# Residual product as four 64x64 blocks, a twentieth home for weight pieces, and three key tiles ahead of the transposes

## The chip, the cores and the metric

One core of a Trainium2 chip runs the whole kernel in one launch. The metric is the device time of that launch in microseconds (us); lower is better. The engines are named as in the profile: PE (TensorE, the matmuls) with PEld (its weight loads), DVE (VectorE), ACT (ScalarE), POOL (GpSimd), SP (SyncE, which here only issues DMAs and waits). All data is float32.

## What is computed

A backbone of two layers over 1024 latent tokens (and 256 context tokens) of width 1024. The parts that the change touches:

```python
# layer 0: windowed attention and a gated linear attention side by side, one output projection
# layer 1: y = W_out(B * conv3(C * W_in x))
for l in range(2):
    h = layer_norm(alpha * h + gate1 * mixer_l(modulate(h)))
    tokens = modulate(h)                                  # 1024 x 1024
    g = argmax(tokens @ wg + bg)                          # one of 4 groups
    e1, e2, w1_, w2_ = top2 of the group's 8 experts      # 32 experts in all
    y = w1_ * ffn[e1](tokens) + w2_ * ffn[e2](tokens)     # ffn = (silu(x W1) * (x W3)) W2
    h = layer_norm(alpha * h + gate2 * y)                 # alpha = 4 ** 0.25
return h[latent]
```

Each expert has W1 and W3 (1024x512) and W2 (512x1024): 6 MB, so that each layer reads 192 pieces of 1 MB (1,048,576 bytes).

## The kernel before

**The order of the work.** Everything is scheduled by hand: each engine has its own list of instructions, and semaphores order them. A layer ends with an expert stage followed by a combining stage.

**The expert stage** (`moe`, on every engine). 21 steps of 128 gathered token rows each. In step b, PE multiplies them by W1 (`hidden_half(b, 0)`, L1291) and by W3 (`hidden_half(b, 1)`), transposes the gathered rows of the next step (`gathered_T`, L818) and the gated hidden rows of the step before (`gated_T`, L1299), and multiplies by W2 (`output`, L1315). POOL gathers the rows of a later step from `h_rows` in DRAM by an indirect DMA (L2560) and scatters the output rows of the step before to `y_rows` (L2565).

**The homes of the pieces.** The weights come in pieces of 1 MB, half of one matrix of one expert. SP issues them in a fixed order (`piece`, L543 is the line of its `load` helper). They live in 19 homes in on-chip memory ("slots", `SLOTS`), 8 KB in each of the 128 partitions. A table that is made when the kernel is built says which home each of the 192 pieces goes to and which earlier piece must have been used up first (`BEFORE`). SP then waits for the semaphore of the product that used that earlier piece (`h_mm` or `y_mm`, L652) before it issues the load; the waits and loads are in one queue, so a late release holds back all that follow. Pieces 0 to 18 have empty homes and are issued while the mixer of the layer still runs, each as soon as the memory of its home is free of other data; number 15 is the last of them. Piece 19 waits for `routed` (DVE has finished sorting the tokens) and for the first quarter of the hidden product of step 0.

**The combining stage** (`combined`, with `residual_part`, L1406 to 1427 on PE). For each of 8 tiles t of 128 tokens, PE adds in PSUM `alpha * h` and the two weighted expert outputs of each token. The first term is `residual_part`: two matmuls of a 128x128 matrix alpha times identity with the 512 columns of one half of the row tile (L1413). The second is four matmuls with 64 output rows each, two beside each other (L1427). A float32 matmul is two records in the profile. Sums of even tiles use the banks 4 and 5 of PSUM, those of odd tiles 0 and 1. `residual_part(t)` waits until ACT has normalized tile t - 2 out of PSUM (`nrm`, L1613). DVE then reads the sum for the LayerNorm statistics (L1990, twice 512 columns), ACT takes the root (L1609), DVE forms reciprocal and shift (L2003, L2005). In layer 0 PE then transposes the normalized tile for the mixer of layer 1 (`stream_T(t - 1)`, L818), DVE and ACT evict the transposes (L1742, L1481), and POOL prepares sums of tokens for the convolution (`token_sums`, L2636 to 2643). In layer 1 POOL multiplies by the LayerNorm weight (L2661), DVE adds the bias (`affine`, L2304) and SP stores the tile.

**Where the rows come from.** During the mixer SP stores the normalized rows to `h_rows`. At the end of the expert stage, SP waits for the last use of home 18, loads the LayerNorm parameters, then loads the rows back in four loads of 1 MB (`ROW_SLOTS` 9, 11, 14, 15; two tiles each), waits for the last scatter and loads the expert outputs (`pair`, eight tiles of 1 MB).

**The attention slots.** The attention and the gated linear attention of layer 0 run in 36 interleaved "slots" (not the homes above). In each slot PE makes the scores (L953) of one pair of heads, transposes probabilities of an earlier pair (`probs_T`, L970), once for each of its two heads, and multiplies values with the pair before that (`values`, L984), over up to five tiles of 128 keys. DVE copies one part of the transposes out of PSUM (L1867), ACT the other (L1557). In the slots with `slot % 4 == 1` the first two key tiles of `values` stand ahead of the first `probs_T`, the others between the two.

Of the kernel before, what the change touches and what calls it, by code (L numbers as in the profile page):

```python
# [12 lines left out]
D, SEQ, CTX, DEPTH = 1024, 1024, 256, 2  # L13
P = 128
# [37 lines left out]
PIECES.sort(key=lambda piece: 0 if piece[2] in STEPS[0] else 1 if piece[2] < FIXED and piece[0] < 2 else 2)  # L52
SLOTS = 19

# [15 lines left out]
ROW_SLOTS = (9, 11, 14, 15)  # L70
ROW_LOADS = [int(n <= 8 or n in ROW_SLOTS) for n in range(SLOTS)]


def filled(slot, l, turn):

    return 16 * ((FILLS[slot] + ROW_LOADS[slot]) * l + turn + 1)

# [77 lines left out]
def program(nc, T, out):  # L155
# [5 lines left out]
    with ctx:  # L161
# [163 lines left out]

        def slot_at(n, q):
            return slot_space(n)[:, D * q:D * (q + 1)] if n >= 12 else blocks[:, SLOT_BLOCKS[n][q], :]

# [212 lines left out]
        def _(sp):  # L541
# [57 lines left out]
            w_in(3)  # L599
            sp.wait_ge(S("wa2_zero"), 1)  # L600
            load(wa2x[0:16, 0:256], T["gla_wa2"][0, 0], "wa2_in")
# [35 lines left out]
            def piece(l, n):  # L637

                m, h, q = PIECES[n]
                if n >= SLOTS:  # L640
                    m_was, h_was, q_was = BEFORE[n]
                    if m_was < 2:
                        sp.wait_ge(S(f"h_mm{l}"), 4 * LAST[q_was] + 2 * m_was + h_was + 1)
                    else:
                        sp.wait_ge(S(f"y_mm{l}"), LAST[q_was] + 1)
                if n == SLOTS:
                    sp.wait_ge(S("routed"), 8 * l + 6)
                src = T[("moe_w1", "moe_w3", "moe_w2")[m]][l].rearrange("e (p h k) n -> p e h (k n)", p=P, h=2)[:, :, h]
                if q < FIXED:
                    src = src[:, q, :]  # L650
                else:
                    e = sp.value_load(order[0:1, q:q + 1], min_val=0, max_val=NE - 1)  # L652
                    src = src[:, bass.ds(e, 1), :].squeeze(1)
                slot = SLOT_OF[m, h, q][0]
                if slot >= 12:
                    dst = slot_space(slot)
                else:
                    b0, b1 = SLOT_BLOCKS[slot]
                    dst = bigA[:, D * b0:D * (b0 + 2)]
                    if b1 != b0 + 1:  # L660
                        dst, src = blocks[:, b0:b1 + 1:b1 - b0, :], src.rearrange("p (b n) -> p b n", b=2)
                load(dst, src, f"w_in_{slot}")

            def store(l, t):
                sp.wait_ge(S("ln"), 2 * l * NT + t + 1)
                sp.dma_start(h_dram[l][t * P:(t + 1) * P, :], hh[:, t]).then_inc(S("h_out"), 16)

            def piece_in_rows(l, n):

                sp.wait_ge(S("h_out"), 16 * ((NT + 1) * l + 2 * (n - 11)))  # L670
                piece(l, n)
# [29 lines left out]
            for l in range(DEPTH):  # L701
# [23 lines left out]
                piece(l, 11)  # L725
                piece_in_rows(l, 15)
                for n in range(SLOTS, len(PIECES)):
                    piece(l, n)
                    if n == WEIGHTS_OUT:
                        sp.wait_ge(S("routed"), 8 * l + 7)  # L730
                        sp.dma_start(w_dram[l], wts[:, :, :].rearrange("p k t -> p (k t)")).then_inc(S("h_out"), 16)
                    if n == WEIGHTS_IN:
                        sp.wait_ge(S("h_out"), 16 * (NT + 1) * (l + 1))
                        w_rows = w_dram[l].rearrange("(h i) (k t) -> i k h t", h=2, k=2)
                        for h in range(2):
                            load(row_w[:, h, :], w_rows[:, :, h, :], "wr_in")
# [9 lines left out]
                for n, slot in enumerate(ROW_SLOTS):  # L746
                    last_use(slot)
                    dst = blocks[:, 12 + 2 * n:14 + 2 * n, :] if n < 2 else hh[:, 2 * n:2 * n + 2]
                    load(dst, h_dram[l][2 * n * P:2 * (n + 1) * P, :].rearrange("(t p) n -> p t n", p=P), f"w_in_{slot}")
                sp.wait_ge(S("routed"), 8 * l + 8)  # L750
# [38 lines left out]
                if l == DEPTH - 1:  # L789
                    for n, t in enumerate([*range(NT - 2), NT - 1, NT - 2]):  # L790
                        sp.wait_ge(S("ln"), (2 * l + 1) * NT + n + 1)
                        sp.dma_start(out[0, t * P:(t + 1) * P, :], hh[:, t]).then_inc(S("out_done"), 16)
                    sp.wait_ge(S("out_done"), 16 * NT)
                    return
# [17 lines left out]
        def _(pe):  # L812
# [290 lines left out]
            for slot in range(SLOTS_ALL):  # L1103
# [3 lines left out]
                gla_second(slot)  # L1107
                split = 2 if slot % 4 == 1 else 0
                if split and 3 <= slot < PAIRS + 3:
# [296 lines left out]
            def residual_part(l, t):  # L1406

                slot = ROW_SLOTS[t // 2]
                pe.wait_ge(S(f"w_in_{slot}"), filled(slot, l, FILLS[slot]))
                if t >= 2:  # L1410
                    pe.wait_ge(S("nrm"), NT * (2 * l + 1) + t - 1)
                for n in range(2):
                    mm(bank(sum_at(t) + n), alpha_i[:, :], row_at[t][:, n * 512:(n + 1) * 512], start=True, stop=False,  # L1413
                       skip_group_check=True)

# [57 lines left out]
        def _(act):  # L1473
# [128 lines left out]
            act.wait_ge(S("ms_ok"), NT // 2)  # L1602
            go(rms, ms, ACT.Sqrt, bias=epsc[:, 1:2], scale=1.0 / DV).then_inc(S("rms_a"), 1)

            def ln(norm, t, src):

                j, n = t % 2, NT * norm + t
                act.wait_ge(S("var"), n + 1)
                go(sd[:, j:j + 1], mv[:, j, 1:2], ACT.Sqrt, bias=epsc[:, 0:1]).then_inc(S("sd"), 1)  # L1609
                if norm % 2 == 0 and t == NT - 1:  # L1610
                    return
                act.wait_ge(S("nmr"), n + 1)
                go(hh[:, t], src, ACT.Identity, bias=nm[:, j:j + 1], scale=rs[:, t:t + 1]).then_inc(S("nrm"), 1)  # L1613
# [115 lines left out]
        def _(dve):  # L1729
            V = Steps(dve, "dve_step")  # L1730
            v = nc.vector
            v.memset(wa2x[:, :], 0.0).then_inc(S("wa2_zero"), 1)
            v.memset(epsc[:, 0:1], LN_EPS)
# [206 lines left out]
            for slot in range(SLOTS_ALL):  # L1940
# [27 lines left out]
                if 2 <= slot < PAIRS + 2:  # L1968
                    probs_out(slot - 2, 1)
            dve.wait_ge(S("rms_a"), 1)  # L1970
            V(v.reciprocal(rms, rms))
# [28 lines left out]
            def ln_scale(norm, t):  # L2000
                j = t % 2
                dve.wait_ge(S("sd"), NT * norm + t + 1)
                V(v.reciprocal(rs[:, t:t + 1], sd[:, j:j + 1]))  # L2003
# [4 lines left out]
            def last_row(l, z):  # L2008

                t, j = NT - 1, (NT - 1) % 2  # L2010
                dve.wait_ge(S("sd"), NT * 2 * l + t + 1)
                v.reciprocal(rs[:, t:t + 1], sd[:, j:j + 1]).then_inc(S("nmr"), 1)
# [468 lines left out]
        def _(pool):  # L2481
# [71 lines left out]
            def moe(l):  # L2553

                pool.wait_ge(S("routed"), 8 * l + 3)
                pool.wait_ge(S("h_out"), 16 * ((NT + 1) * l + NT))

# [129 lines left out]
```

## Time and profile before

| | |
|---|---|
| median of three runs | 2289.83 us (2288.42 to 2290.57) |
| time of the profiled execution | 2290.16 us |
| its span, first to last instruction | 2288.3 us |
| mean granted PE clock | 0.984 of full speed |
| PE busy | 2166.8 us, 95% of the span |
| DVE, ACT, POOL busy | 35%, 18%, 15% |
| DMA, whole span | 572.50 MB, mean 250 GB/s |
| DMA in the expert stages (most slices) | 408 to 420 GB/s |

The expert stage of layer 0 lies at about 757 to 1246 us from the span's start, that of layer 1 at about 1747 to 2234 us; the combining stages follow, at 1260 to 1295 and 2248 to 2286 us. The attention slots lie at about 375 to 592 us. A busy share of PE near 100% does not say that PE bounds: its matmuls are pipelined, and where it waits for a short time the share hides it. What ends last is read from the chain of waits and from single rows.

### The profile page before, as it was taken

Reading aid. Unit: us, or ns where it says so; the run is one execution under the profiler, and the core shown is the slowest. Engines: PE = TensorE matmul, PEld = TensorE weight load, DVE = VectorE, ACT = ScalarE, POOL = GpSimd, SP = SyncE. Lnnn points to the kernel's source line nnn. Section 1 sums busy time; section 2 is a strip of 40 time slices with the busy share of each in tenths; the row PEclk is TensorE's granted clock in tenths of the full one; section 3 lists DMA queues with packets and bytes.
Section 4 is the critical chain, followed back from the end, with each engine's and each line's share of the span. In section 5 each row is a group of like instructions: output and inputs, shape, how many; then the busy total and the mean of one; then the engine's idle time right before and its main releaser. Section 6 shows DMA issues by size and latency. Waiting matters only on the chain. (4 is left out here: it accounts for less than half of the span.)

```text
span 2288.3 us, 27969 instructions
## 1 busy us (share of the span) xinstructions
PE 2166.8 (95%) x10576; PEld 1047.0 (46%) x10576; DVE 808.2 (35%) x1711; ACT 402.3 (18%) x862; POOL 350.7 (15%) x382
## 2 busy tenths in 40 slices
PE   6999999999999999999997999999998999999996
PEld 3547545777554343434432444444553343334431
DVE  2694213656626311111111633334455111111114
ACT  2301042554211110111110500000111111010112
POOL 0000012222131101100100413221320010201003
PEclk8999999999999999999999999999999999999998
DMA  9892000001436999999998411114337999999997
GB/s 388 332 372 81 1 0 1 2 2 39 145 97 246 371 419 419 419 414 419 409 419 350 175 41 52 37 55 165 141 113 279 417 419 419 408 420 419 411 396 296
DMA packets 135816, 572.50 MB, mean 250 GB/s; under 512 B 25049, under 2 KB 38521, under 8 KB 93690
## 3 DMA queue, kind: packets, MB, share of 16 engines
q1 hardware_dynamic: 123002, 537.04, 59.2%
q0 software_dynamic: 12672, 33.57, 3.8%
q8 instruction: 89, 1.46, 0.3%
q14 instruction: 53, 0.43, 0.1%
HBM read 548.52 MB, written 34.62 MB: 255 GB/s over the span
## 5 line engine op out<-in xcount | busy, mean ns | idle before, releaser
L1291 PE MATMUL bank<-bigA,bigB 128*32 128x512 f32 (+2 forms) x1888 | 478.4, 598 | 13.6 <-DMA bigA<-in_moe_w 8.3
L867 PE MATMUL bank<-bigC,bigB 128*128 128x512 f32 (+3 forms) x768 | 293.7, 538 | 0.0
L1291 PEld LDWEIGHTS bank<-bigA,bigB 128*32 128x32 f32 (+2 forms) x1888 | 157.6, 133 | 237.5 <-issue 229.5
L1315 PE MATMUL bank<-bigA,bigB 128*32 128x512 f32 (+2 forms) x912 | 242.5, 594 | 6.3 <-DVE bigB L2241 3.1
L867 PEld LDWEIGHTS bank<-bigC,bigB 128*128 128x128 f32 x768 | 143.4, 194 | 128.4 <-issue 119.8
L1291 PE MATMUL bank<-bigC,bigB 128*32 128x512 f32 (+2 forms) x560 | 171.4, 593 | 0.0
L1367 PE MATMUL bank<-bigB,bigA 128*128 128x512 f32 x384 | 170.7, 592 | 0.0
L1481 ACT ACTIVATE bigB<-bank,small 128x128 f32<-128x128 f32 x280 | 104.3, 459 | 367.1 <-PE bank L818 367.0
L2565 POOL DMA_INDIRECT y_rows<-bigB,ints x42 | 42.3, 1007 | 810.5 <-DVE bigB L2246 810.5
L2246 DVE TENSOR_TENSOR bigB<-bank,gate 128x512 f32<-128x512 f32 x84 | 54.1, 686 | 236.5 <-PE bank L1315 236.5
L2237 DVE TENSOR_TENSOR bigB<-bigB,bank 128x512 f32<-128x512 f32 x42 | 28.9, 688 | 303.8 <-PE bank L1291 303.8
L1315 PEld LDWEIGHTS bank<-bigA,bigB 128*32 128x32 f32 (+2 forms) x912 | 80.3, 135 | 107.0 <-issue 101.9
L1367 PEld LDWEIGHTS bank<-bigB,bigA 128*128 128x128 f32 x384 | 72.8, 190 | 90.9 <-issue 90.9
L1626 ACT ACTIVATE bigB<-bank 128x512 f32<-128x512 f32 x42 | 25.1, 597 | 498.4 <-PE bank L1291 498.4
L1163 PE MATMUL bank<-bigB,bigA 128*128 128x512 f32 x256 | 112.7, 594 | 0.0
L1367 PE MATMUL bank<-bigA 128*128 128x512 f32 x240 | 109.0, 593 | 2.3 <-issue 1.2
L2241 DVE COPY bigB<-bank 128x256 f32<-128x256 f32 x42 | 17.8, 424 | 243.0 <-PE bank L1299 243.0
L1291 PE MATMUL bank<-misc,bigB 128*32 128x512 f32 (+2 forms) x320 | 101.8, 594 | 1.9 <-DMA bigA<-in_moe_w 1.4
L1315 PE MATMUL bank<-bigC,bigB 128*32 128x512 f32 (+2 forms) x400 | 100.8, 594 | 1.8 <-DMA bigA<-in_moe_w 1.8
L1784 DVE SCALAR_TENSOR_TENSOR lnwb<-bigA,misc,lnwb 128x1024 f32<-128x1024 f32 x70 | 89.9, 1284 | 5.1 <-DMA bigA<-in_ada_w 0.8
L1742 DVE TENSOR_SCALAR bigB<-bank,small 128x128 f32<-128x128 f32 x216 | 73.8, 403 | 25.6 <-PE bank L818 23.2
L1291 PEld LDWEIGHTS bank<-bigC,bigB 128*32 128x32 f32 (+2 forms) x560 | 52.4, 128 | 56.1 <-issue 55.4
(351 smaller groups left out, 2597.0 us busy)
## 6 DMA issues: line engine op xcount, KB each, us to landing
bigA<-in_moe_w SPq DMA_DIRECT2D x250, 1024.0 KB, 24.9
bigC<-in_moe_w SPq DMA_DIRECT2D x80, 1024.0 KB
bigA<-in_ada_w SPq DMA_DIRECT2D x40, 1024.0 KB, 6.8
misc<-in_moe_w SPq DMA_DIRECT2D x36, 1024.0 KB, 24.8
lnwb<-in_moe_w SPq DMA_DIRECT2D x18, 1024.0 KB, 25.9
bigA<-y_rows SPq DMA_DIRECT2D x14, 1024.0 KB, 10.7
bigA<-in_w_in_odd SPq DMA_DIRECT2D x12, 1024.0 KB, 5.2
bigA<-in_ada_w SPq DMA_DIRECT2D x4, 2048.0 KB, 13.6
```

Source lines behind the costliest of these rows:

```text
L867: last = mm(bank(n % 3)[:, 0:w], uT[:, k, t * P:(t + 1) * P], wring[:, g % 2, k, at_:at_ + w], start=(k == 0), stop=(k == KC - 1))
L1163: last = mm(bank(2 * ((t + 1) % 2) + n), zT[:, t, k, :], wout1[:, k, n * 512:(n + 1) * 512], start=(k == 0), stop=(k == KC - 1))
L1291: last = mm(bank(m)[at_:at_ + w, :], xT[:, j, KC // 2 * h + k, at_:at_ + w], w13_at(SLOT_OF[m, h, q][0], k), start=(h == 0 and k == 0), st ...
L1315: last = mm(bank(6 + n)[at_:at_ + w, :], gT[:, 2 * h + k, at_:at_ + w], w2_at(SLOT_OF[2, h, q][0], k)[:, n * 512:(n + 1) * 512], start=(h ...
L1367: last = mm(bank(b[s % 2]), lhs[:, k, :], rhs(k), start=(first and k == 0), stop=(k == 3), skip_group_check=True)
L1481: last = go(dst[k], bank(b + k // 4)[:, (k % 4) * P:(k % 4 + 1) * P], ACT.Identity, bias=shift[:, k:k + 1], scale=scale[:, k:k + 1])
L1626: go(sg, bank(0), ACT.Silu).then_inc(S(f"silu_a{l}"), 1)
L1742: last = v.tensor_scalar(dst[k], bank(b + 1)[:, (k - 4) * P:(k - 3) * P], scale[:, k:k + 1], shift[:, k:k + 1], MUL, ADD)
L1784: V(v.scalar_tensor_tensor(acc[:, r % 2], part, cond[:, k, 0:1], acc[:, r % 2], MUL, ADD))
L2237: v.tensor_tensor(gg, sg, bank(1), MUL).then_inc(S(f"g_d{l}"), 1)
L2246: v.tensor_tensor(yo[:, j, n * 512:(n + 1) * 512], bank(6 + n), gate[:, 1, n * 512:(n + 1) * 512], MUL)\
L2565: pool.indirect_dma_start(out=y_dram[l], out_offset=bass.IndirectOffsetOnAxis(ap=rows, axis=0), in_=yo[:, j], in_offset=None, bounds_check ...
```

## The change

There are three edits; the rest joins semaphores into one (`h_out` and `out_done` into `rows_out`, `sd` and `rms_a` into `root`, `wa2_zero` into `dve_step`), which frees their number for the new home and alters no order.

- **Four blocks.** `residual_part` multiplies by the two diagonal 64x64 blocks of alpha times identity. Row half u of the data and column half n give one matmul each; its result goes to output partitions `64 * (u ^ n)`. The four use the four quarters of the array. For this the second column half of the rows must lie with its two halves of 64 partitions swapped, so each of the four row loads becomes three: one of 512 KB (columns 0 to 511) and two of 256 KB (columns 512 to 1023, 64 partitions each). The runs in memory go from 4 KB to 2 KB.
- **A twentieth home.** It is made of `gate[:, 0, :]` (free after the mixer's last residual) and of the end of `bigB` (free once the tokens are sorted), 4 KB a partition each, so a piece there comes in two loads of 512 KB. Piece 19, which is one of an expert known beforehand, now waits for `routed` alone. All later pieces are assigned anew by the same rule.
- **Three key tiles.** In the slots with `slot % 4 == 1`, three key tiles of `values` stand ahead of the first `probs_T` in place of two.

```diff
-SLOTS = 19
+SLOTS = 20
-ROW_LOADS = [int(n <= 8 or n in ROW_SLOTS) for n in range(SLOTS)]
+ROW_LOADS = [3 * (n in ROW_SLOTS) + (n <= 8) for n in range(SLOTS)]
...
-    return 16 * ((FILLS[slot] + ROW_LOADS[slot]) * l + turn + 1)
+    return (32 if slot == SLOTS - 1 else 16) * ((FILLS[slot] + ROW_LOADS[slot]) * l + turn + 1)
...
         def slot_at(n, q):
+            if n == SLOTS - 1:
+                return bigB[:, 9216:10240] if q else gate[:, 0, :]
...
                 slot = SLOT_OF[m, h, q][0]
+                if slot == SLOTS - 1:
+                    for i in range(2):
+                        load(slot_at(slot, i), src[:, D * i:D * (i + 1)], f"w_in_{slot}")
+                    return
...
                 piece_in_rows(l, 15)
+                sp.wait_ge(S("routed"), 8 * l + 6)
+                piece(l, 19)
                 for n in range(SLOTS, len(PIECES)):
...
-                    load(dst, h_dram[l][2 * n * P:2 * (n + 1) * P, :].rearrange("(t p) n -> p t n", p=P), f"w_in_{slot}")
+                    rows = h_dram[l][2 * n * P:2 * (n + 1) * P, :].rearrange("(t p) n -> p t n", p=P)
+                    load(dst[:, :, 0:512], rows[:, :, 0:512], f"w_in_{slot}")
+                    for u in range(2):
+                        load(dst[64 * u:64 * u + 64, :, 512:], rows[64 - 64 * u:128 - 64 * u, :, 512:], f"w_in_{slot}")
...
-                split = 2 if slot % 4 == 1 else 0
+                split = 3 if slot % 4 == 1 else 0
...
-                pe.wait_ge(S(f"w_in_{slot}"), filled(slot, l, FILLS[slot]))
+                pe.wait_ge(S(f"w_in_{slot}"), filled(slot, l, FILLS[slot] + ROW_LOADS[slot] - 1))
...
                 for n in range(2):
-                    mm(bank(sum_at(t) + n), alpha_i[:, :], row_at[t][:, n * 512:(n + 1) * 512], start=True, stop=False,
-                       skip_group_check=True)
+                    for u in range(2):
+                        rows, to = slice(64 * u, 64 * u + 64), 64 * (u ^ n)
+                        mm(bank(sum_at(t) + n)[to:to + 64, :], alpha_i[rows, 64 * u:64 * u + 64], row_at[t][rows, n * 512:(n + 1) * 512],
+                           start=True, stop=False, skip_group_check=True)
```

## Rows read from the trace of the kernel before

**Rows 1.** Windows: us, busy us of each engine, PE clock, DMA share, GB/s.

```profile
2050.00:2100.00 50.00, 50.00 (x150) 22.79 (x149) 7.54 (x16) 4.75 (x12) 4.05 (x4) 1.00 1.02 419
2220.00:2240.00 20.00, 14.72 (x75) 5.44 (x76) 2.91 (x5) 1.67 (x2) 1.99 (x2) 1.00 0.90 354
```

**Rows 2.** Chain that ended last: start us, us, what; end of layer 1's experts.

```profile
2206.01 23.87 DMA bigA<-in_moe_w
...
2235.80 7.66 DMA y_rows<-bigB,ints
```

**Rows 3.** Timeline of SP's DMA issues, around the first releases of both layers.

```profile
757.48 10.20 SPq L543 DMA_DIRECT2D bigA<-in_moe_w  x6
...
1737.89 0.43 SPq L543 DMA_DIRECT2D bigC<-in_moe_w  x1
1747.06 10.20 SPq L543 DMA_DIRECT2D bigA<-in_moe_w  x6
```

**Rows 4.** Windows of 4 us around the same two places.

```profile
1744.00:1748.00 4.00, 4.00 (x22) 1.29 (x18) 1.85 (x8) 0.10 (x1) 0.00 (x0) 1.00 0.07 25
...
756.00:760.00 4.00, 4.00 (x22) 1.42 (x20) 0.22 (x2) 0.00 (x0) 0.00 (x0) 1.00 0.79 260
```

**Rows 5.** Timeline, combining stage of layer 1: start us, us, engine, instruction, [idle before <-releaser].

```profile
2265.09 1.20 ACT L1613 ACTIVATE bigC<-bank,small 128x1024 f32<-128x1024 f32 x1 [0.43 <-DVE small L2005]
2266.43 1.96 PE L1413 MATMUL bank<-bigC,alpha_i 128*128 128x512 f32 x4
2266.52 1.30 DVE L1990 BATCH_NORM_STATS2 small<-bank 128x6 f32<-128x512 f32 x2 [0.34 <-PE bank L1427]
2268.32 1.94 PE L1427 MATMUL bank<-bigA,bigB 128*64 128x512 f32 x8
2270.30 1.30 DVE L1990 BATCH_NORM_STATS2 small<-bank 128x6 f32<-128x512 f32 x2 [0.31 <-PE bank L1427]
```

**Rows 6.** Timeline, combining stage of layer 0.

```profile
1279.81 1.30 DVE L1990 BATCH_NORM_STATS2 small<-bank 128x6 f32<-128x512 f32 x2 [1.07 <-PE bank L1427]
...
1280.69 1.88 PE L1413 MATMUL bank<-bigC,alpha_i 128*128 128x512 f32 x4
...
1284.37 1.16 PE L818 MATMUL bank<-misc,bigC 128*128 128x128 f32 x8
1284.49 1.30 DVE L1990 BATCH_NORM_STATS2 small<-bank 128x6 f32<-128x512 f32 x2 [1.07 <-PE bank L1427]
```

**Rows 7.** Timeline of PE in the attention slots, products on quarters and on the whole array.

```profile
458.20 1.10 PE L1032 MATMUL bank<-bigA,bigC 64*64 64x128 f32 x32
465.20 2.05 PE L1065 MATMUL bank<-bigA,bigC 128*128 128x128 f32 x16
```

**Rows 8.** Timeline behind the combining stage of layer 0.

```profile
1307.36 1.44 POOL L2626 TENSOR_TENSOR bigA<-bigA 128x512 f32<-128x512 f32 x1 [0.24 <-POOL misc L2643]
1310.60 3.70 PE L1367 MATMUL bank<-bigA 128*128 128x512 f32 x8 [1.10 <-DVEq L2379]
```

**Rows 9.** Timeline of one attention slot with slot % 4 == 1.

```profile
454.64 0.74 PE L970 MATMUL bank<-misc,bigB 128*128 128x128 f32 x5 [0.50 <-issue]
455.31 0.88 PE L984 MATMUL bank<-bigB,bigA 128*64 128x128 f32 x12
455.70 0.41 DVE L1867 COPY bigB<-bank 128x256 f32<-128x256 f32 x1
456.25 0.74 PE L970 MATMUL bank<-misc,bigB 128*128 128x128 f32 x5
```

**Rows 10.** Windows: a load with 2 KB runs, the row loads' end, PE's lower clock.

```profile
1574.00:1576.00 2.00, 2.00 (x6) 0.94 (x5) 0.47 (x1) 0.00 (x0) 0.00 (x0) 1.00 1.03 400
2242.00:2244.00 2.00, 0.00 (x0) 0.00 (x0) 0.00 (x0) 0.00 (x0) 0.00 (x0) 1.00 0.26 107
2248.00:2250.00 2.00, 2.00 (x6) 0.46 (x5) 0.00 (x0) 0.00 (x0) 0.00 (x0) 0.50 1.02 397
```

**Rows 11.** Timeline: the first combining product of layer 1, at the lower clock.

```profile
2247.71 3.68 PE L1427 MATMUL bank<-bigA,bigB 128*64 128x512 f32 x8 [7.10 <-DMA bigA<-y_rows]
```

More of the change, by code:

```diff
@@ L599, in _ @@
             w_in(3)
-            sp.wait_ge(S("wa2_zero"), 1)
+            sp.wait_ge(S("dve_step"), 1)
             load(wa2x[0:16, 0:256], T["gla_wa2"][0, 0], "wa2_in")
@@ L665, in store @@
                 sp.wait_ge(S("ln"), 2 * l * NT + t + 1)
-                sp.dma_start(h_dram[l][t * P:(t + 1) * P, :], hh[:, t]).then_inc(S("h_out"), 16)
+                sp.dma_start(h_dram[l][t * P:(t + 1) * P, :], hh[:, t]).then_inc(S("rows_out"), 16)
             def piece_in_rows(l, n):
-                sp.wait_ge(S("h_out"), 16 * ((NT + 1) * l + 2 * (n - 11)))
+                sp.wait_ge(S("rows_out"), 16 * ((NT + 1) * l + 2 * (n - 11)))
                 piece(l, n)
@@ L730, in _ @@
                         sp.wait_ge(S("routed"), 8 * l + 7)
-                        sp.dma_start(w_dram[l], wts[:, :, :].rearrange("p k t -> p (k t)")).then_inc(S("h_out"), 16)
+                        sp.dma_start(w_dram[l], wts[:, :, :].rearrange("p k t -> p (k t)")).then_inc(S("rows_out"), 16)
                     if n == WEIGHTS_IN:
-                        sp.wait_ge(S("h_out"), 16 * (NT + 1) * (l + 1))
+                        sp.wait_ge(S("rows_out"), 16 * (NT + 1) * (l + 1))
                         w_rows = w_dram[l].rearrange("(h i) (k t) -> i k h t", h=2, k=2)
@@ L791, in _ @@
                         sp.wait_ge(S("ln"), (2 * l + 1) * NT + n + 1)
-                        sp.dma_start(out[0, t * P:(t + 1) * P, :], hh[:, t]).then_inc(S("out_done"), 16)
-                    sp.wait_ge(S("out_done"), 16 * NT)
+                        sp.dma_start(out[0, t * P:(t + 1) * P, :], hh[:, t]).then_inc(S("rows_out"), 16)
+                    sp.wait_ge(S("rows_out"), 16 * (DEPTH * (NT + 1) + NT))
                     return
@@ L1602, in _ @@
             act.wait_ge(S("ms_ok"), NT // 2)
-            go(rms, ms, ACT.Sqrt, bias=epsc[:, 1:2], scale=1.0 / DV).then_inc(S("rms_a"), 1)
+            go(rms, ms, ACT.Sqrt, bias=epsc[:, 1:2], scale=1.0 / DV).then_inc(S("root"), 1)
             def ln(norm, t, src):
@@ L1608, in ln @@
                 act.wait_ge(S("var"), n + 1)
-                go(sd[:, j:j + 1], mv[:, j, 1:2], ACT.Sqrt, bias=epsc[:, 0:1]).then_inc(S("sd"), 1)
+                go(sd[:, j:j + 1], mv[:, j, 1:2], ACT.Sqrt, bias=epsc[:, 0:1]).then_inc(S("root"), 1)
                 if norm % 2 == 0 and t == NT - 1:
@@ L1731, in _ @@
             v = nc.vector
-            v.memset(wa2x[:, :], 0.0).then_inc(S("wa2_zero"), 1)
+            V(v.memset(wa2x[:, :], 0.0))
             v.memset(epsc[:, 0:1], LN_EPS)
@@ L1969, in _ @@
                     probs_out(slot - 2, 1)
-            dve.wait_ge(S("rms_a"), 1)
+            dve.wait_ge(S("root"), 1)
             V(v.reciprocal(rms, rms))
@@ L2001, in ln_scale @@
                 j = t % 2
-                dve.wait_ge(S("sd"), NT * norm + t + 1)
+                dve.wait_ge(S("root"), NT * norm + t + 2)
                 V(v.reciprocal(rs[:, t:t + 1], sd[:, j:j + 1]))
@@ L2010, in last_row @@
                 t, j = NT - 1, (NT - 1) % 2
-                dve.wait_ge(S("sd"), NT * 2 * l + t + 1)
+                dve.wait_ge(S("root"), NT * 2 * l + t + 2)
                 v.reciprocal(rs[:, t:t + 1], sd[:, j:j + 1]).then_inc(S("nmr"), 1)
@@ L2555, in moe @@
                 pool.wait_ge(S("routed"), 8 * l + 3)
-                pool.wait_ge(S("h_out"), 16 * ((NT + 1) * l + NT))
+                pool.wait_ge(S("rows_out"), 16 * ((NT + 1) * l + NT))
                 def gather(j, rows):
```

## The prediction, made before the changed kernel was run

> **What bounds the kernel now.** I read the page's totals first: PE is busy for 95% of the span. That does not tell the two expert stages apart from the rest, so next came windows over them. In the middle of layer 1's stage PE is busy for all of 50 us and the DMA engines move 419 GB/s at the same time; in its last 20 us PE is busy for only 14.72 us [rows 1]. So both run at their limit for long stretches, and the end tells which is later. The chain that ended last goes through a weight piece that took 23.87 us from issue to landing [rows 2]. At 419 GB/s a piece of 1,048,576 bytes takes 2.50 us, so nine pieces stood before it in the DMA queues: SP issued it early enough, and the bytes themselves were late. The stage is bound by its DMA stream, which runs from the first release to the last piece. A megabyte that moves before the first release is worth 2.50 us, if the engines are idle then.
>
> Behind the experts the chain goes through the last scatter, the first load of expert outputs, and then PE, tile by tile. In layer 1 a statistics instruction starts every 3.78 us (2266.52 to 2270.30); DVE is idle for only 0.31 us of it, and the two PE rows of a tile, 1.89 us and 1.9 us from start to start, fill it all [rows 5]. PE bounds, DVE is 0.31 us behind. In layer 0 PE has three things per tile, the residual of 1.88 us, the product and the transposes of 1.16 us; the statistics start every 4.68 us (1279.81 to 1284.49), and DVE waits 1.07 us of them for PE [rows 6].
>
> **Four blocks, price of one.** Now the four records of the residual take 1.89 us from the start of the first to the next product, 0.47 each [rows 5]. The new form has eight records of 512 columns. The trace has quarters of the array at work in the attention slots: 32 records of 128 columns in 1.10 us, against 16 records of the same length on the whole array in 2.05 us [rows 7]. That is 0.034 against 0.128 us each, a factor of 3.7. So eight records cost 8 x 0.47 / 3.7 = 1.02 us: 0.87 us less per tile. The bounds are no gain (1.89) and full overlap (0.94).
>
> **Layer 0.** The residuals of tiles 0 and 1 are done while PE waits for expert outputs, and save nothing. Tiles 2 to 7 each shorten PE's round by 0.87 us, from 4.68 to 3.81. DVE needs 4.68 - 1.07 = 3.61 us per tile, so it stays just behind PE. Six tiles give 5.2 us. What is late next is the convolution's first product that needs the token sums, at 1310.60. It waited for DVE [rows 8], whose part begins when the last tile is evicted, so it moves the whole 5.2 us, to 1305.4. POOL's part ended at 1307.36 + 1.44 = 1308.8 and begins with the fifth tile, so it moves by only four tiles, 3.5 us, to 1305.3. The two meet; I book all 5.2 us and keep 1 us for a loss here.
>
> **Layer 1.** PE's round falls to 2.91 us, but DVE's own takes 3.78 - 0.31 = 3.47 us. The loop through the normalization is not longer: from statistics to the end of ACT's pass 3.57 us (2265.09 + 1.20, less the start one round of 3.80 us before 2266.52), 0.14 to the residual's start, 1.02, 1.95 for the product, 6.7 us for two tiles or 3.36 per tile. So DVE takes over. The pipeline starts with slack on DVE: the statistics of tile 3 come the full 0.87 us earlier, and the four tiles after it 0.31 each. Together 2.1 us. The last tile's way to the store is unchanged.
>
> **The twentieth home.** In layer 1 SP issued piece 15 at 1737.89 and then waited for the first hidden product until 1747.06 [rows 3]. The DMA engines moved 25 GB/s from 1744 to 1748 [rows 4]: against 419, (419 - 25) x 4 us = 1.58 MB were not moved, and piece 19 fits whole. Its wait, for `routed`, is over at about 1740 (I put it where SP's issue still falls ahead of the gap). The stream is ahead by 2.50 us from then on. In layer 0 piece 15 was late, for it waited for a row store, and the idle part from 756 to 760 holds (419 - 260) x 4 = 0.64 MB, 1.5 us [rows 4]. Piece 19 goes there; piece 20 is issued at 757.48 as 19 was [rows 3] and queues behind it. So 4.0 us in all. All 172 later pieces get their release one earlier than now or the same, so no wait of SP grows. Nothing is behind the new wait for `routed` that could go sooner: piece 20 needed it already. The ten more loads per layer on SP's queue (0.3 to 0.5 us each to issue) lie inside a backlog of 24 us. A further gain is possible where all engines ran dry for a moment in the middle of a stage; I take none, and keep 2 us of it for the range, because only some of the engines are idle then and the slowest decides when a piece has landed.
>
> **The row loads.** Twelve loads in place of four, with runs of 2 KB. A load of W_out with such runs moved 400 GB/s [rows 10], 5% less than 419. 4.2 MB then take 10.5 in place of 10.0 us. The row loads end between 2242 and 2244, where only 107 GB/s move [rows 10], and SP can't issue the expert outputs before the scatter has landed, at 2235.80 + 7.66 = 2243.46 [rows 2]. So half a microsecond is nearly covered; the scatter shares the engines with the loads for a little longer. I take 0.2 us per layer; the bounds are 0 and, if the covered time is gone and the runs move at half the rate, 7.5 us. SP's eight more issues, some 0.5 us each, end ten microseconds before its next wait does.
>
> **Three key tiles.** Ahead of the first transposes PE is idle for 0.50 us [rows 9]; one key tile costs 0.88 / 3 = 0.29 us and fits. But the second set of transposes starts at 456.25, and what it waits for is DVE's copy, which ends at 455.70 + 0.41 = 456.11; the products between end at 456.19. With one tile fewer between, PE waits there in place of working. I take nothing. With eight such slots the bounds are 8 x 0.29 = 2.3 us either way: a gain if DVE's copy moved too, a loss in the slots that have no idle time.
>
> **The sum.** 5.2 + 2.1 + 4.0 - 0.4 = 10.9 us. The profiled execution took 2290.16 us, so 2279.3; the median of the runs lies 0.33 us below it: 2279.0 us. The joined semaphores have the same counts at the same places and cost nothing.
>
> **Rivals.**
> *A. Row halves of one bank take turns, slower.* Every product on row halves in this trace sends each row half to a PSUM bank of its own (L1032, L1053, L953 by their code). In the new residual both row halves write into one bank, in different partitions. No row shows this. If two such matmuls can't run together, the second waits for the first, the third (another bank) runs beside the second, the fourth waits: three steps of 0.945 us, 2.84 in place of 1.89. It decides as soon as the residual is longer than 1.89 us, for PE sets the period in both stages: 0.95 x 6 tiles x 2 layers = 11.4 us lost, less 4.0 from the home, plus 0.4: 2297.6. For it speaks only that the kernel never did it before; against it, that column halves of one bank do run beside each other (L1427: eight records in 1.94 us, [rows 5]).
> The Trainium skill states this rule: "Different row tiles cannot access same PSUM bank simultaneously" (TensorEngine Tiling (Array Packing), Gotcha 1: PSUM Pressure). Whether it means also different partitions of the bank, it does not say, and no row here tests it.
> *B. Two at a time.* The four blocks overlap only in pairs, 1.89 us as before: the stages gain nothing, 2290.16 - 0.33 - 4.0 + 0.4 = 2286.2.
> *C. The expert stage is PE's.* For it: PE busy for 50 of 50 us [rows 1]. Against it: the end of the stage, as above. The home would be worth nothing: 2283.0.
> *D. The clock stays low.* The first combining product of layer 1 took 3.68 us, after a wait of 7.10 us for data, with a granted clock of 0.50, the level of 1.2 GHz [rows 10, 11], against 1.94 later [rows 5]. With PE busy for 2.9 of 3.5 us the clock might stay there: 3.68 + 2.04 = 5.72 us per tile against 3.78, 11.6 us for six tiles, and the 2.1 are gone: 2292.7. Against it: with 14.72 of 20 us busy the granted clock was full [rows 1].
> *E. More than forecast.* The dry moments are filled, or the key tiles gain: 2275 or below.
>
> **Chances.** Forecast, 2275.5 to 2282.5: 0.57. E 0.13, C 0.10, B 0.09, A 0.07, D 0.04. The range that should hold the time 8 times in 10 goes from 2273.5, most of E, to 2286.5, with C and B. Changes under 0.2%, 4.6 us, can't be told from none: faster means below 2285.3. Faster: 0.57 + 0.13 + 0.10 = 0.80; same, B and D: 0.13; slower, A: 0.07.
>
> **What would show it.** Four blocks: the new line's records on 64*64, eight of them within about 1.0 us, products of a tile 2.9 us after each other where nothing waits; A would show them in three steps. Layer 0: statistics 3.8 us apart. Layer 1: 3.5 us apart, DVE without idle time. Home: SP's issue of 512 KB pairs ahead of the first release, the hole of 25 GB/s filled, and the last weight piece 2.5 and 1.5 us earlier against the first release of its layer. Row loads: the time from the last scatter to the expert outputs unchanged. Key tiles: idle time moves from the first to the second transposes, and the slots keep their length. The prediction is wrong if the first release itself moves later, if blocks take turns, or if POOL's token sums end later than 1305.5.

## The result and the profile after

The changed kernel takes 2295.5 us (median of 13 runs, 2292.78 to 2300.11), the kernel before 2289.83 (13 runs beside it): 1.0027 times, 95% interval 1.0019 to 1.0035. It is 5.7 us slower, where I forecast 10.8 us faster. Single profiled executions differ by up to 3 us where nothing has changed yet (the start of the layer-0 experts lies between 1.6 us earlier and 3.0 us later than in the trace of before), so below I take differences between two places of one trace, and only then between traces.

The chain of waits of the changed kernel, at the place of [rows 2]:

```profile
2206.19 22.79 DMA bigA<-in_moe_w
...
2234.89 10.76 DMA y_rows<-bigB,ints
2245.68 7.97 DMA bigA<-y_rows
2253.78 3.69 PE bank L1440 x8
```

The last scatter took 10.76 us to land in place of 7.66, and the first combining product begins 8.10 us behind the issue of the expert outputs (2245.68 to 2253.78), where it was 4.23 (2243.48 to 2247.71 [rows 2, 11]). The windows of [rows 1, 4, 10] on the changed kernel, and one in layer 0 (time, then busy us of PE, PEld, DVE, ACT, POOL, granted clock, DMA share, GB/s):

```profile
2220.00:2240.00 20.00, 11.81 (x72) 4.06 (x68) 2.91 (x5) 1.67 (x2) 1.99 (x2) 0.93 0.94 269
1744.00:1748.00 4.00, 3.78 (x18) 1.35 (x20) 2.72 (x9) 1.27 (x1) 0.00 (x0) 1.00 1.00 388
756.00:760.00 4.00, 4.00 (x22) 1.43 (x20) 0.61 (x4) 0.00 (x0) 0.00 (x0) 1.00 0.99 394
1250.00:1252.00 2.00, 1.63 (x2) 0.00 (x0) 0.00 (x0) 0.00 (x0) 0.00 (x0) 0.50 1.10 229
2242.00:2244.00 2.00, 0.69 (x4) 0.00 (x0) 0.00 (x0) 0.00 (x0) 0.00 (x0) 0.50 1.07 372
2248.00:2250.00 2.00, 0.00 (x0) 0.00 (x0) 0.00 (x0) 0.00 (x0) 0.00 (x0) 0.50 1.02 310
```

Read the last two columns together. The holes of 25 and 260 GB/s are filled, 388 and 394. But around the row loads the engines are busy all the time (share 1.10) and move 229 GB/s: busy, and at half the rate. SP's issues, each line's length running from the start of its first to the end of its last (start, us; layer 1, then layer 0):

```profile
2222.87 0.34 SPq L545 DMA_DIRECT2D lnwb<-in_ln_w  x1
...
2223.73 5.00 SPq L545 DMA_DIRECT2D bigA<-h_rows  x6
2228.78 9.42 SPq L545 DMA_DIRECT2D bigC<-h_rows  x6
2245.68 11.37 SPq L545 DMA_DIRECT2D bigA<-y_rows  x9
...
1235.77 4.17 SPq L545 DMA_DIRECT2D bigA<-h_rows  x6
1239.99 7.50 SPq L545 DMA_DIRECT2D bigC<-h_rows  x6
1257.60 9.63 SPq L545 DMA_DIRECT2D bigA<-y_rows  x9
```

The twelve issues last 14.5 us in layer 1; the four of before lasted 2.3 us. That is no sign of the half rate: in experiment 2 eight loads with runs of 2 KB, which move at 400 GB/s, keep SP for 9.9 us, and eight into 64 partitions with rows of 4 KB, which move at 236, for 5.5. What the twelve loads cost is read from the GB/s and from the start of the first product.

The combining stages, as [rows 5, 6], on all engines; layer 1, then layer 0:

```profile
2268.27 1.28 DVE L2003 BATCH_NORM_STATS2 small<-bank 128x6 f32<-128x512 f32 x2
2268.53 2.35 POOL L2674 TENSOR_TENSOR bigC<-bigC,lnwb 128x1024 f32<-128x1024 f32 x1 [1.33 <-ACT bigC L1626]
2268.59 1.09 PE L1426 MATMUL bank<-bigC,alpha_i 64*64 64x512 f32 x8 [0.73 <-ACT bigC L1626]
2269.61 1.94 PE L1440 MATMUL bank<-bigA,bigB 128*64 128x512 f32 x8
2270.42 0.47 DVE L2018 SCALAR_TENSOR_TENSOR small<-small 128x1 f32<-128x1 f32 x1
2270.82 1.21 DVE L2317 TENSOR_TENSOR bigC<-bigC,lnwb 128x1024 f32<-128x1024 f32 x1
2271.95 1.28 DVE L2003 BATCH_NORM_STATS2 small<-bank 128x6 f32<-128x512 f32 x2
...
1282.25 1.30 DVE L2003 BATCH_NORM_STATS2 small<-bank 128x6 f32<-128x512 f32 x2 [0.37 <-PE bank L1440]
1283.22 1.09 PE L1426 MATMUL bank<-bigC,alpha_i 64*64 64x512 f32 x8
1284.24 1.94 PE L1440 MATMUL bank<-bigA,bigB 128*64 128x512 f32 x8
1286.11 1.16 PE L829 MATMUL bank<-misc,bigC 128*128 128x128 f32 x8
1286.23 1.30 DVE L2003 BATCH_NORM_STATS2 small<-bank 128x6 f32<-128x512 f32 x2 [0.37 <-PE bank L1440]
```

The eight block records take 1.02 us from start to the next product, as forecast. Layer 0 has a round of 3.98 us (forecast 3.81), layer 1 one of 3.68 (forecast 3.47).

### The profile page after: what moved, and what is told of

Same layout as the page of the kernel before. It is cut to its first block and busy times, and to the rows that moved or that the text cites. A ratio compares the mean times of both kernels' runs of the same rounds, so it can differ in the third digit from the quotient of the medians.

```text
span 2293.7 us, 28169 instructions
## 1 busy us (share of the span) xinstructions
PE 2160.0 (94%) x10640; PEld 1042.0 (45%) x10640; DVE 809.7 (35%) x1711; ACT 402.8 (18%) x862; POOL 350.9 (15%) x382
## 5 line engine op out<-in xcount | busy, mean ns | idle before, releaser
L1302 PE MATMUL bank<-bigA,bigB 128*32 128x512 f32 (+2 forms) x1856 | 465.3, 596 | 12.0 <-DMA bigA<-in_moe_w 6.4
L1326 PE MATMUL bank<-bigA,bigB 128*32 128x512 f32 (+2 forms) x896 | 227.7, 594 | 4.3 <-DMA bigA<-in_moe_w 1.8
L1302 PE MATMUL bank<-bigC,bigB 128*32 128x512 f32 (+2 forms) x448 | 137.4, 602 | 0.0
L1302 PE MATMUL bank<-misc,bigB 128*32 128x512 f32 (+2 forms) x336 | 118.3, 605 | 6.6 <-DMA bigA<-in_moe_w 6.6
L1326 PE MATMUL bank<-bigC,bigB 128*32 128x512 f32 (+2 forms) x368 | 93.1, 594 | 3.1 <-DMA lnwb<-in_moe_w 2.6
L1378 PEld LDWEIGHTS bank<-bigA 128*128 128x128 f32 x240 | 45.4, 190 | 60.7 <-issue 60.7
```

Of the source, the lines that this page charges most:

```text
L1302: last = mm(bank(m)[at_:at_ + w, :], xT[:, j, KC // 2 * h + k, at_:at_ + w], w13_at(SLOT_OF[m, h, q][0], k), start=(h == 0 and k == 0), st ...
L1326: last = mm(bank(6 + n)[at_:at_ + w, :], gT[:, 2 * h + k, at_:at_ + w], w2_at(SLOT_OF[2, h, q][0], k)[:, n * 512:(n + 1) * 512], start=(h ...
L1378: last = mm(bank(b[s % 2]), lhs[:, k, :], rhs(k), start=(first and k == 0), stop=(k == 3), skip_group_check=True)
```

## The experiments

Theory P: a load into 64 partitions keeps all DMA engines busy but moves half as much, and this alone makes the change slower. Its rivals: the runs of 2 KB, the number of transfers, the blocks themselves, or the home. The kernels were timed in three series: experiments 1 and 2; 3, 4, 5 and 8; 6, 7 and the second run of 4. In each the kernel before ran on the same chip, with a median of 2289.4 to 2289.9; the chips of the three series differ. So where kernels of two series are compared, the difference of each to its own runs of before is what counts.

**1. Old residual and old loads, home and key tiles kept.** The residual's and the row loads' hunks of the diff are undone.

> The changed kernel with the residual of before (four products on the whole array) and the four row loads of before; the twentieth home and the three key tiles stay. Theory P (a load into 64 partitions moves at half the rate, and the row loads lose more than the rest gains): the row loads move at over 380 GB/s again, the expert outputs are issued some 2.5 us after where the home alone puts them, and the time is 2290 - 4.7 (home, from the two first releases against the two normalization loads in the traces) = 2285. Theory B (the blocks or their longer dependence on POOL cost time elsewhere): also 2285. Theory H (the home costs what it gains, because its loads take bandwidth from the stream): 2290, no change.

Measured: 2288.95 us, ratio 0.9996 (0.9987 to 1.0005), 0.5 below the kernel before. The loss is gone, so it is in the loads or the blocks; theories P and B both say so, and this run can't part them. But the expected gain of 4.7 is hardly there (theory H is not excluded by this run; see 5 and 7).

**2. The shape of the loads.** Three kernels with the blocks, each home's rows loaded in another shape:

```diff
-load(dst[:, :, 0:512], rows[:, :, 0:512], ...)
-for u in range(2):
-    load(dst[64*u:64*u+64, :, 512:], rows[64-64*u:128-64*u, :, 512:], ...)
+load(dst, rows, ...)                                              # one load
+for c in range(2): load(dst[:, :, 512*c:512*c+512], ...)          # 2 KB runs
+for u in range(2): load(dst[64*u:64*u+64], rows[64*u:64*u+64], ...)  # 64 partitions
```

> The changed kernel with its four blocks, but each home's rows loaded by one transfer over all 128 partitions as before, so that the second column half of the residual is taken from the other 64 tokens of the tile (that part of the output is another one). Theory P: the stream is that of the kernel before, and the blocks add their gain to the home's: 2285 - 6 x 0.70 (period of layer 0, 4.68 to 3.98) - 1 (layer 1) = 2280. Theory B: the blocks' gain in the stages is given back behind them, 2285 or more.

> As the one with one load per home, but two loads per home, each of one column half over all 128 partitions, in runs of 2 KB; the second half again from the other 64 tokens. Theory P: rate near 400 GB/s, time within 1.5 us of the one-load kernel, 2280 to 2282. Theory R (runs of 2 KB move at half the rate when they come from these rows): as the changed kernel, 2293 to 2296, with 210 to 250 GB/s.

> As the one with one load per home, but two loads per home, each into 64 partitions, with whole rows of 4 KB; the second column half from the other 64 tokens. Theory P: all 4.2 MB of a layer move at 210 to 250 GB/s in place of half of them, so 2293 to 2298, as slow as the changed kernel or slower. Theory R (runs of 2 KB): rate near 400 GB/s, 2280. Theory N (the number of transfers, three per home): between them by two thirds of the way back, about 2285.

Measured: 2523.46, 2524.91 and 2540.72 us. The totals I expected were all wrong by some 240 us. These kernels leave out the exchange of the token halves, so layer 0's output is another one, and with it the experts that layer 1's tokens go to: behind the row loads of layer 1 SP issues 18 more loads of expert weights, over 208.58 us with one load per home, for tokens above the planned number. The three stand beside each other only, and up to the end of layer 0 beside the rest. One load and runs of 2 KB are alike; 64 partitions cost 16 to 17 us, of which 6.6 are there in layer 0 already. SP's issues of layer 0, runs of 2 KB over 128 partitions:

```profile
1234.22 2.30 SPq L545 DMA_DIRECT2D bigA<-h_rows  x4
...
1252.93 6.56 SPq L545 DMA_DIRECT2D bigA<-y_rows  x9
```

and 4 KB rows into 64 partitions:

```profile
1235.98 2.69 SPq L545 DMA_DIRECT2D bigA<-h_rows  x4
...
1261.65 6.50 SPq L545 DMA_DIRECT2D bigA<-y_rows  x9
```

From the first row load to the expert outputs: 19.0 us before (1236.41 to 1255.43), 19.0 with one load, 18.7 with runs of 2 KB, 21.8 in the changed kernel (2 MB into 64 partitions), 25.7 with all 4 MB into 64. Windows of those two kernels:

```profile
1246.00:1248.00 2.00, 1.07 (x2) 0.19 (x3) 0.00 (x0) 0.00 (x0) 0.38 (x1) 1.00 1.05 400
```

```profile
1250.00:1252.00 2.00, 0.00 (x0) 0.00 (x0) 0.00 (x0) 0.00 (x0) 0.99 (x1) 1.00 1.05 236
```

The same number of transfers, the same share of 1.05, 400 against 236 GB/s, and runs of 2 KB on the fast side: it is the 64 partitions, neither the runs nor the count. One thing these three leave open is the changed kernel's own shape, twelve loads with runs of 2 KB and 64 partitions in one: from the first row load to the first combining product of layer 0 its 2 MB into 64 partitions cost 5.2 us (28.4 for 23.2), while 4 MB in eight loads cost 6.6 (29.9 for 23.3). My estimate for 2 MB, at 229 in place of 400 GB/s, is 3.9 us. No run shows what the rest is.

**3. The new loads alone**, with the four products on the whole array (the second half not exchanged):

```diff
-    load(dst[64*u:64*u+64, :, 512:], rows[64-64*u:128-64*u, :, 512:], ...)
+    load(dst[64*u:64*u+64, :, 512:], rows[64*u:64*u+64, :, 512:], ...)
```

> The loads of the change alone, with the residual of before: each home's rows in one load of the first column half over 128 partitions and two of the second into 64 partitions, not exchanged, for four products on the whole array; home and key tiles as in the changed kernel. Theory P: the loss of the loads stands without the blocks' gain: 5.2 us (layer 0) and 7.0 us (layer 1) over the kernel with the old loads and the old residual, so 2289 + 12 = 2301. Theory B (the blocks' matmuls make the first products late): as with the old loads, 2289.

Measured: 2298.98 us, ratio 1.0037 (1.0023 to 1.0051), 9.1 us above the kernel before. The kernel of experiment 1, which differs in nothing but these loads, was 0.5 below it. So the price of the loads is 9.6 us, with 3 to 4 us of doubt either way. The blocks, which the changed kernel has beside this one, take 3.4 us back (5.7 above the kernel before in place of 9.1).

**4. The changed kernel with an exchanged copy in DRAM**, so that no row load is narrower than 128 partitions:

```diff
+h_swap = [nc.dram_tensor(f"h_swap{l}", [SEQ, 512], ...) ...]
 def store(l, t):
     sp.dma_start(h_dram[l][t*P:(t+1)*P, :], hh[:, t]) ...
+    for u in range(2):
+        sp.dma_start(h_swap[l][t*P+64*u:t*P+64*u+64, :], hh[64-64*u:128-64*u, t, 512:]) ...
...
+load(dst[:, :, 0:512], rows[:, :, 0:512], ...)
+load(dst[:, :, 512:], h_swap rows, ...)
```

> The changed kernel with all three of its parts, but the second column half of the rows is also stored to DRAM with the two token halves of each tile exchanged, at the time of the row stores, and each home's rows then come in two loads over all 128 partitions. Theory P (loads into 64 partitions move at half the rate, and that is all that is wrong): rows at some 400 GB/s, first products of both combining stages as early as with the old residual. By the differences in the traces so far: home 0.7 + 1.6, blocks 4.2 in layer 0 and 0.7 in layer 1, so 2289.5 - 7.2 = 2282.3; the 2 MB of stores more per layer fall at the end of the mixer, and cost up to 1 us in layer 0, where the DMA engines move 286 GB/s in the last 20 us. Theory S (what is late is the number of transfers on SP's queue or the blocks themselves, so the loss stays): 2290 or more.

> The kernel with the swapped copy once more, beside the one with the early read: 2282 to 2286, by its first runs.

Measured: 2284.14 us, ratio 0.9973 (0.9964 to 0.9983), and 2284.97 us, ratio 0.9982 (0.9973 to 0.9991), in the third series. It beats the kernel before by 4.5 to 5.8 us and the changed one by 10 to 11. Its row loads move 389 to 410 GB/s, and its outputs are issued 18.4 us behind the first row load (2220.92 to 2239.34). Theory S falls. I had expected 2 us more; what is missing is in the home and in the two stages, below.

**5. The same with nineteen homes.** The hunks of the home are undone.

> The same as the one with the swapped copy, but with nineteen homes as before. By my prediction the home is worth 4.0 us, so 4.0 us more than the one with the home; by the traces so far 2.3 us more; theory H (a home more doesn't move the end of a stage that is bound elsewhere): equal.

Measured: 2287.38 us, ratio 0.9990 (0.9981 to 0.9999), 3.2 us above its counterpart of the same series; between experiment 1 and the kernel before it was 0.5 us. Home and stream in the traces: from SP's first released weight load to its load of the norm's parameters, layer 1 took 476.74 us before (1747.06 to 2223.80 in [rows 3] and the same view) and 474.05 in the changed kernel (1748.82 to 2222.87), 2.69 shorter; layer 0 478.07 and 476.03, 2.04 shorter. That is 4.7 us, as much as I had said and more. But this stretch is shorter in part because it started later. PE's first hidden products, and SP's first released loads, before:

```profile
753.79 7.09 PE L1291 MATMUL bank<-bigA,bigB 128*64 128x512 f32 x32 [0.73 <-ACT bigB L1481]
```

and in the changed kernel:

```profile
754.22 7.09 PE L1302 MATMUL bank<-bigA,bigB 128*64 128x512 f32 x32 [0.74 <-ACT bigB L1494]
...
758.88 8.11 SPq L545 DMA_DIRECT2D bigA<-in_moe_w  x5
```

Before, the load followed after 3.69 us (757.48 [rows 3]); now after 4.66. In layer 1 it is 3.70 (1743.36 to 1747.06) and 4.60 (1744.22 to 1748.82). Piece 19 belongs to an expert fixed in advance, piece 20 to one chosen at run time, and SP reads its number from SBUF between the wait and the load. Both wait for the same product.

What counts is the whole stretch, from PE's first hidden products to the norm's parameters (us; the last two rows are experiment 6):

| kernel | products to first released load, layers 0 and 1 | products to the norm's parameters, layers 0 and 1 | sum |
|---|---|---|---|
| before, 19 homes | 3.69, 3.70 | 481.76, 480.44 | 962.2 |
| exchanged copy, 19 homes | 3.73, 3.73 | 481.53, 480.02 | 961.6 |
| changed | 4.66, 4.60 | 480.69, 478.65 | 959.3 |
| old residual (experiment 1) | 4.66, 4.94 | 481.29, 479.12 | 960.4 |
| exchanged copy (experiment 4) | 4.66, 4.61 | 481.42, 479.08 | 960.5 |
| exchanged copy, early read | 3.86, 3.86 | 480.82, 477.95 | 958.8 |
| old residual, early read | 3.86, 4.19 | 481.30, 478.46 | 959.8 |

All three traces with 19 homes (that of experiment 7 is the third) give 962.0 in the mean (961.6 to 962.2), all six with twenty homes and the late read 960.1 (959.3 to 960.6): the home is worth 1.9 us net.

**6. The expert number read ahead of the wait**, with the exchanged copy and with the old residual:

```diff
 m, h, q = PIECES[n]
+if n == SLOTS: sp.wait_ge(S("routed"), 8 * l + 6)
+e = None if q < FIXED else sp.value_load(order[0:1, q:q+1], ...)
 if n >= SLOTS:
     ... sp.wait_ge(...)                # the home is free
-    e = sp.value_load(order[0:1, q:q+1], ...)
```

> As the one with the swapped copy, but SP reads a piece's expert number before it waits for the home, not behind the wait. With twenty homes the first piece that waits is one of an expert chosen at run time, and in the traces its transfer is issued 4.66 us (layer 0) and 4.60 us (layer 1) after PE's first hidden products begin, where with nineteen homes it is of a fixed expert and comes at 3.69 and 3.70 us. Theory I (this read is why the home brings 2.2 us in place of 4.0): first issues at 3.7 us again, each layer's experts 0.9 us shorter, 2284.1 - 1.9 = 2282.2. Theory J (the home's gain is lost in the stage, on PE or in the DMA queues): 2284, no change.

> Home and key tiles on the old residual with its old loads, the expert number read ahead of the wait. By my prediction's value of a home, 4.0 us less than before: 2285.6. Without the early read the same kernel took 2289.0. Theory I: 2285.5 to 2287.5, first transfers issued 3.7 us after the first hidden products begin. Theory J: as without it.

Measured: 2283.12 us, ratio 0.9969 (0.9960 to 0.9979), 1.85 below its counterpart in the same series (experiment 4, second run), and 2287.01 us, ratio 0.9993 (0.9984 to 1.0002), 1.9 below experiment 1, each against its own runs of before. The intervals overlap (and against the exchanged copy's first run, with its own runs of before, the gain is only 0.6 us), so the medians alone don't settle it; but both pairs differ by the 1.9 us expected, and the trace shows the first load's step. With the exchanged copy:

```profile
1739.56 7.09 PE L1305 MATMUL bank<-bigA,bigB 128*64 128x512 f32 x32 [0.73 <-ACT bigB L1497]
...
1743.42 4.87 SPq L546 DMA_DIRECT2D bigA<-in_moe_w  x4
```

3.86 us, and 3.86 in layer 0 too (754.83 to 758.69). That is 0.7 to 0.8 us earlier per layer, not the whole 0.9, and with the old residual layer 1 stays at 4.19. In the table's sum the exchanged copy with the early read is 1.2 us (against its second run, 960.0) to 1.7 us (against its first) shorter than without, and the old residual 0.6, less than the medians say. Theory J, no change, falls by the pair of one series; how much of the 1.9 us the read is worth stays open between 0.6 and 1.9. With the exchanged copy this is the fastest version that does the whole computation.

**7. Key tiles alone**, in the kernel before: `split = 3`.

> The kernel before with three key tiles in place of two ahead of the transposes, and nothing else. The traces show the idle time move from the first to the second transposes, with slots of the same length: 0 us, within 0.2%. A rival, that each of the eight slots loses or gains a product's share, gives 2.3 us either way.

Measured: 2290.07 us, ratio 1.0002 (0.9993 to 1.0011). Nothing, and no loss.

**8. POOL's multiplication cut short in layer 1's last stage**, with the exchanged copy. The kernel leaves out the norm's weight on 1008 of 1024 columns of these tiles:

```diff
-pool.tensor_tensor(hh[:, t], hh[:, t], lnw, MUL)
+pool.tensor_tensor(hh[:, t, 0:16], hh[:, t, 0:16], lnw[:, 0:16], MUL)
```

> As the one with the swapped copy, but POOL's multiplication with the norm's weights in layer 1's last stage works on 16 columns of 1024 (the rest of the output stays unmultiplied). Theory L (DVE's short instruction on the scale ends only when POOL's 2.35 us are over, which holds the period of layer 1 at 3.69 in place of the 3.47 forecast): that instruction takes 0.16 in place of 0.46 us, statistics start 3.4 to 3.5 us apart, and the whole is 1 to 2 us faster than the one with the swapped copy. Theory M (DVE waits for ACT or PE there): the period stays at 3.69, and so does the time.

Measured: 2282.55 us, ratio 0.9970 (0.9958 to 0.9982), 1.6 below experiment 4's first run, from the same series. Its trace:

```profile
2266.15 1.29 DVE L2006 BATCH_NORM_STATS2 small<-bank 128x6 f32<-128x512 f32 x2
2266.41 0.22 POOL L2677 TENSOR_TENSOR bigC<-bigC,lnwb 128x16 f32<-128x16 f32 x1 [3.15 <-ACT bigC L1629]
...
2268.31 0.16 DVE L2021 SCALAR_TENSOR_TENSOR small<-small 128x1 f32<-128x1 f32 x1
2268.38 1.22 DVE L2320 TENSOR_TENSOR bigC<-bigC,lnwb 128x1024 f32<-128x1024 f32 x1
2269.52 1.29 DVE L2006 BATCH_NORM_STATS2 small<-bank 128x6 f32<-128x512 f32 x2
```

DVE's small instruction takes 0.16 in place of 0.47 us, and the round is 3.37 us. The medians alone would not carry a difference of 1.6 us; the instruction's length does, and five rounds 0.31 us shorter make 1.6.

## Why the prediction was wrong

**The row loads: the step that failed.** I wrote "A load of W_out with such runs moved 400 GB/s" and took 0.2 us per layer. That load went over 128 partitions [rows 10]; I matched the length of the runs and not the partitions. In place of 0.4 us over both layers the loads cost 9.6 by experiments 1 and 3; the upper bound I gave, half the rate and 7.5 us per layer, 15, was nearer. In the traces of before and after it is 3.1 us to the issue of the expert outputs and 3.9 from there to the first product in layer 1, 7.0; and 2.8 and 2.4 in layer 0, 5.2. These 12.2 lie within the doubt of the 9.6. The cover that I named, the scatter's wait, was not there, for the scatter and the first load of expert outputs got slower with the row loads: 10.5 to 10.8 and 7.8 to 8.0 us in the two kernels with loads into 64 partitions (the changed one and experiment 3), 7.2 to 7.8 and 4.0 to 4.2 in the one before and in three without them (experiments 1, 4 and 6). The trace of before would have told. Part of layer 0's W_out is loaded at 548.53, in two loads of 64 partitions each, with runs of 4 KB, and the window shows it:

```profile
551.00:553.00 2.00, 2.00 (x17) 1.59 (x17) 2.00 (x17) 0.42 (x1) 0.37 (x2) 1.00 1.05 229
```

A share of 1.05 at 229 GB/s, the very numbers of the changed kernel. My share column was read only for idle engines, never for busy ones that move little. The Trainium skill has the rule (SBUF — State Buffer, "Door 1: The DMA port swizzle"): partitions 0 to 63 reach the eight even DMA ports of SBUF and 64 to 127 the eight odd ones. The 236 against 400 GB/s of experiment 2 agree with it.

**Four blocks: right in mechanism, too large in size.** Eight records in 1.02 us, so rivals A and B fall: both row halves write different partitions of one bank at once. The rule that I quoted for rival A (TensorEngine Tiling (Array Packing), Gotcha 1, of the Trainium skill) does not hold here, where the two row halves write different partitions of a bank: the measurement decides. In layer 0 the gain is 0.70 us per tile and 4.2 in all, not 0.87 and 5.2. The old residual took 1.81 us from its start to the product's there (1280.69 to 1282.50), not the 1.89 that I had taken from layer 1, and the transposes' step grew from 0.99 to 1.09 (1286.11 to 1287.20). In the run with the exchanged copy the first statistics stand 1.50 us behind those of before and the last 2.71 ahead, 4.2; behind the convolution's first sets the next product is 2.4 ahead (1308.25 for 1310.60), so 0.4 is lost there, inside the 1 us that I kept for it. That product now waits for POOL. My sign that POOL's token sums would end after 1305.5 came true: they end at 1308.10 in that run. Counted from the first statistics that is 2.2 us sooner than before (44.6 for 46.8), not 3.5.

In layer 1 the round is 3.68, not 3.47, and the stage gains 0.7, not 2.1. I had computed that DVE would take over, and it did, but not that it would be held: its L2018 lasts until POOL's multiplication ends (2268.53 + 2.35 = 2270.88, L2018 2270.42 + 0.47 = 2270.89). Before, while PE kept the round at 3.78, the same instruction (L2005) began just as POOL ended, and took 0.16 us:

```profile
2266.37 2.35 POOL L2661 TENSOR_TENSOR bigC<-bigC,lnwb 128x1024 f32<-128x1024 f32 x1 [1.43 <-ACT bigC L1613]
2268.70 0.16 DVE L2005 SCALAR_TENSOR_TENSOR small<-small 128x1 f32<-128x1 f32 x1
```

Experiment 8 shows it. The rule of the Trainium skill (SBUF — State Buffer, "SBUF: two separate sides": of a DVE instruction with two SBUF inputs and a GpSimd instruction that reads SBUF, the first holds their shared port pair to its end, and the other waits) agrees with those two ends.

**The home: half of it.** "Piece 20 is issued at 757.48 as 19 was" was wrong: against PE's first products it came 0.97 us later in layer 0 and 0.90 in layer 1. Net the home brought 2.9 us in the changed kernel's trace and 1.9 in the mean of six. Rival C falls, for the stage did get shorter. With the early read it brings 3.2 and 2.2 us, of which layer 1 gives 2.3 and 1.8 and layer 0 0.9 and 0.4. So in layer 0, where I filled an idle part of 1.5 us, it stayed short of the forecast even then; no run shows why.

**Key tiles: right.** The idle time moved from the first to the second transposes, 0.28 us each where there were 0.50 and none [rows 9], and the slot kept its 1.61 us:

```profile
455.69 0.74 PE L981 MATMUL bank<-misc,bigB 128*128 128x128 f32 x5 [0.28 <-issue]
456.36 0.66 PE L995 MATMUL bank<-bigB,bigA 128*64 128x128 f32 x8
456.74 0.41 DVE L1880 COPY bigB<-bank 128x256 f32<-128x256 f32 x1
457.30 0.74 PE L981 MATMUL bank<-misc,bigB 128*128 128x128 f32 x5 [0.28 <-DVE bigB L1880]
```

**Rival D** did not come: behind the first two tiles the products take 1.94 us again.

**The sum.** The two traces add up, change for change, where the medians only step from kernel to kernel (less 0.5, plus 9.6, less 3.4, which makes 5.7 by construction):

| stretch, changed against before | us |
|---|---|
| start to the first hidden products | +0.4 |
| experts, to the norm's parameters, layers 0 and 1 | -1.1, -1.8 |
| first row load to first combining product, layers 0 and 1 | +5.2, +7.0 |
| layer 0, from there to the convolution's first product that needs the token sums | -3.6 |
| layer 1, from there to the end | -0.7 |
| sum; the spans are 2293.7 and 2288.3 | +5.4 |

So the blocks brought 4.3 of 7.3 us and the home 2.9 of 4.0, and the loads cost 12.2 in place of 0.4.

## What to carry to other kernels

Match a transfer by its partitions before its run length: read DMA share and GB/s side by side, and look for a load of the same shape in the trace. Where data has to change partition halves, exchange them at a store with time to spare, and load over all 128 partitions. A prefetch slot more is worth its bytes only if the next load behind the wait is as ready as the old one; a read of a run-time number belongs ahead of the wait.

## What the runs showed that I had not expected

- Busy engines (share 1.02 to 1.10) at 213 to 245 GB/s in windows of 2 us for loads into 64 partitions, against 387 to 411 over 128.
- Both row halves of the array write different partitions of one bank at once: eight records of 512 columns in 1.09 us.
- A DVE instruction on one column takes 0.47 in place of 0.16 us while POOL multiplies 1024 columns, and ends with it.
- Where SP reads the expert number between the wait and the load, the load comes 0.9 to 1.0 us later than for a fixed expert; with the number read ahead, 0.7 to 0.8 of it go away.
